# One decoder step on one core: the first projection with features on the partitions and 320 moving tokens, turned back by transposes

## The chip, the cores and the metric

The kernel runs on one core of a Trainium2 chip. The metric is device time in microseconds (us), the median of several executions; lower is better. One more execution was taken with the hardware profiler, and all rows below are from it. The engines are PE (TensorE; its weight loads are listed apart as PEld), DVE (VectorE), ACT (ScalarE), POOL (GpSimd) and SP (SyncE, which here only issues DMAs).

## What is computed

One layer of a hybrid decoder for 256 prompt tokens and 8 x 8 sample tokens, 320 in all. The first step is the normalised input times `w_in`; attention, a recurrent branch, the merge and a gated feed-forward network follow.

```python
p = rms_norm(x, norm_g) @ w_in
p_q, p_cmp, p_sel, p_win, p_gate, p_shift, p_merge = jnp.split(p, _splits(PROJ_SIZES), axis=-1)
q = partial_rope(rms_norm(p_q.reshape(B, T, N_HEADS, HEAD_DIM), q_gain), pos)
kv_cmp = kv_rows(p_cmp, k_gains[0], pos)      # likewise kv_sel, kv_win
gates = jax.nn.sigmoid(p_gate.reshape(B, T, N_HEADS, 3))
```

The change concerns the first 2608 columns of `w_in`: q (1024), the three key/value parts (512 each) and the gates (48). Queries and keys are normalised and rotated per head, along the features of a token, so this kernel wants them with tokens on the partitions.

## The kernel before

The stage is `project_qkv`. The columns are cut into 11 chunks, ten of 256 columns and the last (chunk 10) of 48 (`width`). The contraction of 2048 is cut into 16 slices of 128 (`KD`), four to a group, so chunk c has the groups 4c to 4c+3, 44 in all. A group is 128 x 4 x 256 numbers of `w_in`, 512 KB. It goes through the class `Parts`, which has four slots: SP loads it (`load`, L218), ACT rounds it to `hi` (`round`, L224), DVE makes the remainder `lo` (`cut`, L228), PE multiplies. A product in fp32 quality is three matmuls, hi x hi, and the two mixed ones (`three_passes`, L340). The order of each engine is that of its code; semaphores hold it back: a load waits for the `cut` that freed its slot four groups earlier, a `round` for its load and for the matmuls of the group four earlier (`used`), a `cut` for its `round`, and PE for the `cut` of the group (`split`). In the first chunk DVE also normalises the input, slice by slice, into `nH` and `nL` (L356, L361), and PE waits for those slices.

The tokens are the stationary operand: for each of the three token tiles (128, 128, 64, `TOK`) and each of four slices, three matmuls move 256 weight columns, 36 matmuls to a group. The results lie as token rows in banks 3(c%2) + t. ACT's `take(c)` copies the three of them into `pkv` (L556), or, for chunk 10, puts them through the sigmoid into `gates` (L558), after it has rounded the groups of chunk c+1. For the seven chunks in `NORMED` DVE then does `norm_and_rotate` (L595 to L609), and ACT gives the square root in the middle of it (`root`, L562); DVE does this after its cuts of chunk c+1.

SP loads the groups in order; behind group 12 it issues eight copies from DRAM to DRAM (L524, some 1 MB each, `cache_kv_win` into the output), and after the last load `store_rows` writes the key/value rows out, each part after its chunks are taken and rotated; the last part (win) is ten DMAs (L510, L517). The stage ends with a barrier of all engines: SP comes to it after its stores have landed. The stage behind it (`prompt_setup`) begins with DMAs of SP (L648) and copies of POOL (L711).

The product as the changed kernel makes it stands in the kernel already, as `tile_pair`, for the other projections: weights stationary (128 of their columns), all 320 tokens moving, 24 matmuls to a group of 256 columns. Its results have features on the partitions.

Of the kernel before, what the change touches and what calls it, by code (L numbers as in the profile page):

```python
# [44 lines left out]
P = 128  # L45
# [93 lines left out]
class Steps:  # L139
# [10 lines left out]
    def turn(self):  # L150
        assert self.cursor == len(self.names), self.names[self.cursor:]
        self.cursor = 0
# [93 lines left out]
def _layer(nc, a, o, top):  # L246
# [7 lines left out]
    def sem(name):  # L254
        s = scope[0].enter_context(nc.semaphore(name))
        if scope[0] is early:
            early_sems.append(s)
        return s

    def settled(eng):  # L260

        eng.sem_inc(passed, 1)
# [220 lines left out]
    def project_qkv():  # L483
        v = Carve(work, w.at)
        sqr = v(3, 4, HD)
        ss, rt, rs = v(3, 4), v(3, 4), v(3, 4)
        rope = v(4, 3, 4, 8)
        normed, halved, lowered = sem("n1_normed"), sem("n1_halved"), sem("n1_lowered")
        taken, cleared, low_out = sem("qkv_taken"), sem("qkv_cleared"), sem("qkv_low_out")
        norm_sq, rooted, ready, stored = sem("qkv_sq"), sem("qkv_root"), sem("qkv_ready"), sem("qkv_stored")  # L490
        wv = a["w_in"].rearrange("l (k p) c -> p (l k) c", p=P)
        NCH = 11
        NORMED = (0, 1, 2, 3, 4, 6, 8)

        def width(c):
            return 256 if c < 10 else 48

        with nc.Block() as block:
            @block.sync
            def _(sp):  # L500
                def store_rows(j):

                    name = ("cmp", "sel", "win")[j]
                    sp.wait_ge(ready, 5 + j)
                    sp.wait_ge(taken, 3 * (6 + 2 * j))
                    for t, (t0, n) in enumerate(TOK):
                        src = pkv[0:n, t, ATT + j * KVC:ATT + (j + 1) * KVC]
                        if t < 2:
                            dst = o["kv_%s_prompt" % name][0, 0, t0:t0 + n].rearrange("t c g d -> t (c g d)")
                            sp.dma_start(dst, src).then_inc(stored, 16)  # L510
                        elif name != "win":
                            dst = o["kv_%s_sample" % name].rearrange("l b t c g d -> (l b t) (c g d)")
                            sp.dma_start(dst, src).then_inc(stored, 16)
                        else:
                            for b in range(DB):
                                dst = o["kv_win_sample"][0, b, WIN - TS:WIN].rearrange("t c g d -> t (c g d)")
                                sp.dma_start(dst, src[b * TS:(b + 1) * TS, :]).then_inc(stored, 16)  # L517

                for g in range(4, 4 * NCH):
                    c, n = g // 4, width(g // 4)  # L520
                    parts.load(sp, 0, g, wv[:, g % 4 * 4:g % 4 * 4 + 4, c * 256:c * 256 + n], n)
                    if g == 12:
                        for b in range(DB):
                            sp.dma_start(o["kv_win_sample"][0, b, 0:WIN - TS].rearrange("t c g d -> t (c g d)"),  # L524
                                         a["cache_kv_win"][0, b, TS:WIN].rearrange("t c g d -> t (c g d)")).then_inc(win_stores, 16)
                for j in range(3):
                    store_rows(j)
                sp.wait_ge(stored, 16 * (3 * 2 + 2 + DB))
                sp.wait_ge(win_stores, 16 * DB)

            @block.tensor
            def _(pe):
                parts.start_use(pe)
                for g in range(4 * NCH):
                    c, n = g // 4, width(g // 4)
                    parts.ready(pe, 0, g)
                    if g < 4:
                        pe.wait_ge(lowered, 4 * g + 4)
                    if g % 4 == 0 and c >= 2:

                        pe.wait_ge(taken, 3 * (c - 1))
                    for t, (t0, m) in enumerate(TOK):
                        for kk in range(4):
                            k = g % 4 * 4 + kk
                            last = three_passes(bank[3 * (c % 2) + t][0:m, 0:n], parts.hi[:, g % 4, kk, 0:n], parts.lo[:, g % 4, kk, 0:n],
                                                nH[:, k, t0:t0 + m], nL[:, k, t0:t0 + m], False, k == 0, k == KD - 1)
                    last.then_inc(parts.used, 1)

            @block.scalar
            def _(act):  # L550
                def take(c):
                    parts.done(act, 0, 4 * c + 3)
                    for t, (t0, m) in enumerate(TOK):
                        src = bank[3 * (c % 2) + t][0:m, 0:width(c)]
                        if c < 10:
                            nc.scalar.copy(pkv[0:m, t, c * 256:(c + 1) * 256], src).then_inc(taken, 1)  # L556
                        else:
                            nc.scalar.activation(gates[0:m, t, :], src, ACT.Sigmoid).then_inc(taken, 1)  # L558

                def root(c):  # L560
                    act.wait_ge(norm_sq, NORMED.index(c) + 1)
                    nc.scalar.activation(rt, ss, ACT.Sqrt, bias=const("eps")[:, 0:1], scale=1.0 / HD).then_inc(rooted, 1)  # L562

                norm_high(act, parts, full1, normed, halved)
                act.wait_ge(cleared, 1)
                for c in range(NCH):

                    for g in range(4 * c, 4 * c + 4) if c else ():
                        parts.round(act, 0, g, width(c))
                    if c >= 1:  # L570
                        take(c - 1)
                        if c - 1 in NORMED:
                            root(c - 1)
                take(NCH - 1)

            @block.gpsimd
            def _(pool):

                nc.gpsimd.memset(pkv[64:P, 2, :], 0.0).then_inc(cleared, 1)
                pool.dma_start(x_kept, xT[:, :, :]).then_inc(low_out, 16)  # L580
                pool.wait_ge(lowered, KD)
                pool.dma_start(low_dram, nL[:, :, :]).then_inc(low_out, 16)
                pool.wait_ge(low_out, 32)

            @block.vector
            def _(dve):
                own = Chain(dve, sem("qkv_dve"))
                tt = nc.vector.tensor_tensor
                norm_parts(dve, parts, full1, nL, "norm1_g", rstd1, normed, halved, lowered)

                def norm_and_rotate(c):
                    n = NORMED.index(c)
                    dve.wait_ge(taken, 3 * c + 3)
                    x = pkv[:, :, c * 256:(c + 1) * 256].rearrange("p t (h d) -> p t h d", d=HD)
                    own(tt(sqr, x, x, ALU.mult))  # L595
                    nc.vector.tensor_reduce(ss, sqr, AX.X, ALU.add).then_inc(norm_sq, 1)
                    dve.wait_ge(rooted, n + 1)
                    own(nc.vector.reciprocal(rs, rt))
                    own(tt(x, x, rs.unsqueeze(3).to_broadcast([P, 3, 4, HD]), ALU.mult))
                    gain = gains[:, max(n - 3, 0):max(n - 3, 0) + 1, :].unsqueeze(2).to_broadcast([P, 3, 4, HD])  # L600
                    own(tt(x, x, gain, ALU.mult))
                    cos, sin = (const("rope", 3, 2, 8)[:, :, j:j + 1, :].to_broadcast([P, 3, 4, 8]) for j in range(2))
                    x1, x2 = x[:, :, :, 0:8], x[:, :, :, 8:16]
                    own(tt(rope[:, 0], x1, cos, ALU.mult))
                    own(tt(rope[:, 1], x2, sin, ALU.mult))
                    own(tt(rope[:, 2], x2, cos, ALU.mult))
                    own(tt(rope[:, 3], x1, sin, ALU.mult))
                    own(tt(x1, rope[:, 0], rope[:, 1], ALU.subtract))
                    tt(x2, rope[:, 2], rope[:, 3], ALU.add).then_inc(ready, 1)  # L609
                    dve.wait_ge(ready, n + 1)  # L610

                for c in range(NCH):
                    for g in range(4 * c, 4 * c + 4) if c else ():
                        parts.cut(dve, 0, g, width(c))
                    if c - 1 in NORMED:
                        norm_and_rotate(c - 1)

    project_qkv()
    products.close()
# [2151 lines left out]
```

## Time and profile before

| | us |
|---|---|
| median of 3 executions | 3189.82 |
| lowest, highest | 3187.14, 3193.31 |
| the profiled execution, its time | 3192.92 |
| its span in the trace | 3191.1 |
| first matmul of `project_qkv` | 57.51 |
| last one starts | 262.81 |
| SP's first DMA behind the barrier | 263.78 |

The profiled execution has 1.8 us outside the span and lies 3.1 us above the median. PE is busy for 90% of the span, DVE 45%, ACT 30%, POOL 14%. Busy shares are means over stages of different kinds, so the part below goes through the stage itself: when each engine does what, and what it had waited for. Times in the rows are us from the start of the span; a matmul's own duration is longer than the step from one matmul to the next, since they are pipelined, so steps are read from starts.

### The profile page before, as it was taken

To read this page: it belongs to the slowest core of one execution; us is meant where nothing else is said; L and a number is where in the kernel's file an instruction comes from. 1 tells how busy PE (TensorE), PEld (TensorE's weight loads), DVE (VectorE), ACT (ScalarE), POOL (GpSimd) and SP (SyncE) were. 2 spreads that over 40 slices of the span, in tenths; PEclk is the share of its full clock that TensorE was granted. 3 is DMA by queue.
4 is the path that set the end of the run, shared out by engine and by line. 5 is a ranking of instruction groups with operands and counts; after the bars stand their busy time and mean duration, and the time that the engine had idled before them with its cause. 6 is when DMAs were issued, how large, how long until landed. Compare 5 with 4: busy or idle time off the path is not lost. (4 is left out here: it accounts for less than half of the span.)

```text
span 3191.1 us, 52572 instructions
## 1 busy us (share of the span) xinstructions
PE 2874.9 (90%) x18491; PEld 2449.2 (77%) x18491; DVE 1424.1 (45%) x2693; ACT 959.1 (30%) x1914; POOL 441.6 (14%) x584
## 2 busy tenths in 40 slices
PE   6898878887869969999999979898999989999999
PEld 4896654444449958778777857576999989999999
DVE  4542432423325435555555521005666643566643
ACT  3223322222223333333333311002444333344332
POOL 0000013422400013332332300000000000000000
PEclk9995558888879979999999989998999999999999
DMA  5730016546436512222222254432545444444453
GB/s 171 236 108 10 0 53 192 164 145 183 146 122 180 142 33 64 61 66 63 64 60 64 65 166 148 131 118 79 152 140 155 137 140 151 133 153 146 126 161 111
DMA packets 369287, 378.21 MB, mean 119 GB/s; under 512 B 37114, under 2 KB 329037, under 8 KB 367897
## 3 DMA queue, kind: packets, MB, share of 16 engines
q1 hardware_dynamic: 363444, 359.23, 38.2%
q0 software_dynamic: 1296, 13.11, 1.1%
q10 hardware_dynamic: 4438, 4.40, 0.5%
q8 instruction: 71, 1.16, 0.2%
q14 instruction: 38, 0.31, 0.0%
HBM read 356.99 MB, written 27.94 MB: 121 GB/s over the span
## 5 line engine op out<-in xcount | busy, mean ns | idle before, releaser
L228 DVE TENSOR_TENSOR ffn_lo<-ffn_raw,ffn_hi 128x1024 fp32r<-128x1024 f32 x264 | 319.6, 1223 | 366.1 <-ACT ffn_hi L224 365.8
L340 PE MATMUL banks<-n_hi,ffn_hi 128*128 128x320 f32 x1408 | 437.6, 311 | 15.9 <-DVE ffn_lo L228 15.8
L224 ACT CAST ffn_hi<-ffn_raw 128x1024 fp32r<-128x1024 f32 x264 | 275.6, 1048 | 557.7 <-PE banks L340 525.2
L340 PE MATMUL banks<-n_lo_ffn,ffn_hi 128*128 128x320 f32 x1408 | 436.3, 310 | 0.0
L340 PE MATMUL banks<-n_hi,ffn_lo 128*128 128x320 f32 x1408 | 436.2, 310 | 0.0
L340 PEld LDWEIGHTS banks<-n_hi,ffn_hi 128*128 128x128 f32 x1408 | 265.4, 189 | 17.5 <-issue 17.3
L340 PEld LDWEIGHTS banks<-n_lo_ffn,ffn_hi 128*128 128x128 f32 x1408 | 265.5, 189 | 0.0
L340 PEld LDWEIGHTS banks<-n_hi,ffn_lo 128*128 128x128 f32 x1408 | 265.4, 188 | 0.0
L340 PE MATMUL banks<-g_hi,ffn_hi 128*128 128x320 f32 x704 | 220.0, 313 | 13.5 <-DVE ffn_lo L228 13.5
L2010 POOL TENSOR_TENSOR gate_low<-work,gate_high 128x512 fp32r<-128x512 f32 x128 | 166.8, 1304 | 462.4 <-ACT gate_high L1889 462.4
L340 PE MATMUL banks<-g_lo,ffn_hi 128*128 128x320 f32 x704 | 219.1, 311 | 0.0
L340 PE MATMUL banks<-g_hi,ffn_lo 128*128 128x320 f32 x704 | 219.1, 311 | 0.0
L340 PE MATMUL banks<-n_hi,gate_high 128*128 128x320 f32 x512 | 187.2, 366 | 19.5 <-ACT work L1894 18.7
L340 PE MATMUL banks<-qkv_hi,n_hi 128*128 128x256 f32 (+3 forms) x528 | 151.9, 288 | 18.3 <-DVE qkv_lo L228 18.3
L340 PE MATMUL banks<-n_lo_shift,gate_high 128*128 128x320 f32 x512 | 160.0, 312 | 0.0
L340 PE MATMUL banks<-n_hi,gate_low 128*128 128x320 f32 x512 | 160.0, 312 | 0.0
L2330 PE MATMUL banks<-work,ring_out 128*128 128x320 f32 x512 | 140.3, 438 | 14.0 <-DMA ring_out<-w_out 14.0
L340 PE MATMUL banks<-qkv_lo,n_hi 128*128 128x256 f32 (+3 forms) x528 | 151.6, 287 | 0.0
L340 PE MATMUL banks<-qkv_hi,n_lo_qkv 128*128 128x256 f32 (+3 forms) x528 | 151.4, 287 | 0.0
L340 PEld LDWEIGHTS banks<-g_hi,ffn_hi 128*128 128x128 f32 x704 | 133.7, 190 | 14.0 <-issue 14.0
L2330 PEld LDWEIGHTS banks<-work,ring_out 128*128 128x128 f32 x512 | 98.5, 193 | 55.8 <-issue 16.0
L340 PEld LDWEIGHTS banks<-g_lo,ffn_hi 128*128 128x128 f32 x704 | 133.7, 190 | 0.0
(389 smaller groups left out, 5734.3 us busy)
## 6 DMA issues: line engine op xcount, KB each, us to landing
ffn_raw<-w_up SPq DMA_DIRECT2D x176, 512.0 KB, 3.7
ffn_raw<-w_down SPq DMA_DIRECT2D x88, 512.0 KB, 3.6
ring_attention<-cache_kv_sel SPq DMA_DIRECT2D x128, 256.0 KB, 2.9
work<-w_in SPq DMA_DIRECT2D x128, 256.0 KB, 2.9
work<-cache_kv_cmp SPq DMA_DIRECT2D x96, 256.0 KB, 2.9
shift_raw<-w_in SPq DMA_DIRECT2D x48, 512.0 KB, 3.7
qkv_raw<-w_in SPq DMA_DIRECT2D x40, 512.0 KB, 4.2
ring_out<-w_out SPq DMA_DIRECT2D x16, 1024.0 KB, 5.3
```

The lines of the kernel that those rows point to most:

```text
L224: self.nc.scalar.copy(self.hi[:, j % 4, :, 0:n], self.raw[:, j % 4, :, 0:n]).then_inc(self.rounded, 1)
L228: self.nc.vector.tensor_tensor(self.lo[:, j % 4, :, 0:n], self.raw[:, j % 4, :, 0:n], self.hi[:, j % 4, :, 0:n].bitcast(F32), ALU.subtract ...
L340: ins = nc.tensor.matmul(out, lhs, rhs, start=first and n == 0, stop=last and n == 2)
L2010: nc.gpsimd.tensor_tensor(gate_low[n % 4][:, :, :], gate_raw[n % 4], gate_high[n % 4][:, :, :].bitcast(F32), ALU.subtract).then_inc(gate_c ...
L2330: last = nc.tensor.matmul(bank[g][:, 0:NT], slots[:, c, k, h * P:(h + 1) * P], mT[:, c % 2 * 8 + k, :], start=c % 2 == 0 and k == 0, stop= ...
```

## The change

Chunks 0 to 9 are multiplied with `tile_pair` into banks 0 to 3 (two for each chunk), 24 matmuls of 320 columns to a group. Chunk 10 takes 12 matmuls to a group, 48 weight columns stationary and 320 tokens moving. ACT's new `hold(c)` copies the two feature tiles into `byfeat`; PE's new `turn(c)` transposes them, six transposes to a chunk, into banks 4 to 7; ACT's `take(c)` then makes two copies from there instead of three (128 x 2 x 256 and 64 x 256). PE does `turn(c)` after the matmuls of chunk c+1. ACT and DVE do `take`, `root` and `norm_and_rotate` of a chunk one chunk later than before.

```diff
             def _(pe):
                 parts.start_use(pe)
-                for g in range(4 * NCH):
...
-                    for t, (t0, m) in enumerate(TOK):
-                        for kk in range(4):
-                            k = g % 4 * 4 + kk
-                            last = three_passes(bank[3 * (c % 2) + t][0:m, 0:n], parts.hi[:, g % 4, kk, 0:n], parts.lo[:, g % 4, kk, 0:n],
-                                                nH[:, k, t0:t0 + m], nL[:, k, t0:t0 + m], False, k == 0, k == KD - 1)
-                    last.then_inc(parts.used, 1)
+                def turn(c):
+                    pe.wait_ge(held, c + 1)
+                    if c >= 2:
+                        pe.wait_ge(taken, 2 * (c - 1))
+                    settled(pe)
+                    m = min(P, width(c))
+                    for i in range(2 if c < 10 else 1):
+                        for t, (t0, n) in enumerate(TOK):
+                            out = bank[4 + c % 2][0:n, 256 * t + P * i:256 * t + P * i + m] if t < 2 else bank[6 + c % 2][0:n, P * i:P * i + m]
+                            last = nc.tensor.transpose(out, byfeat[0:m, c % 2 * 2 + i, t0:t0 + n], ident[0:m, 0:m])
+                    last.then_inc(turned, 1)
+
+                for c in range(NCH):
+                    for g in range(4 * c, 4 * c + 4):
+                        if g < 4:
+                            pe.wait_ge(lowered, 4 * g + 4)
+                        if g % 4 == 0 and c >= 2:
+                            pe.wait_ge(held, c - 1)
+                        if c < 10:
+                            tile_pair(pe, parts, 0, g, bank[2 * (c % 2):2 * (c % 2) + 2], nL)
+                        else:
...
+                                last = three_passes(bank[0][0:48, 0:NT], parts.hi[:, g % 4, kk, 0:48], parts.lo[:, g % 4, kk, 0:48],
+                                                    nH[:, k, :], nL[:, k, :], True, k == 0, k == KD - 1)
...
+                    if c:
+                        turn(c - 1)
+                turn(NCH - 1)
             @block.scalar
+                def hold(c):
+                    parts.done(act, 0, 4 * c + 3)
+                    m = min(P, width(c))
+                    for i in range(2 if c < 10 else 1):
+                        last = nc.scalar.copy(byfeat[0:m, c % 2 * 2 + i, :], bank[2 * (c % 2) + i][0:m, 0:NT])
+                    last.then_inc(held, 1)
+
                 def take(c):
-                    parts.done(act, 0, 4 * c + 3)
...
+                    act.wait_ge(turned, c + 1)
...
                     if c >= 1:
-                        take(c - 1)
-                        if c - 1 in NORMED:
-                            root(c - 1)
+                        hold(c - 1)
+                    if c >= 2:
+                        take(c - 2)
+                        if c - 2 in NORMED:
+                            root(c - 2)
+                hold(NCH - 1)
+                take(NCH - 2)
                 take(NCH - 1)
             @block.vector
-                    if c - 1 in NORMED:
-                        norm_and_rotate(c - 1)
+                    if c - 2 in NORMED:
+                        norm_and_rotate(c - 2)
             @block.sync
-                    sp.wait_ge(taken, 3 * (6 + 2 * j))
+                    sp.wait_ge(taken, 2 * (6 + 2 * j))
```

How the rows stand on DVE, at the passage from chunk 0 to chunk 2, before: `L228` is a cut, `L595` and `L596` begin `norm_and_rotate(0)`.

```order
L228 TENSOR_TENSOR qkv_lo<-qkv_raw,qkv_hi 128x1024 [waits parts_rounded] x5
L595 TENSOR_TENSOR work<-work 128x768 [waits qkv_taken]
L596 TENSOR_REDUCE work<-work 128x12 [waits qkv_dve]
L598 RECIPROCAL work<-work 128x12 [waits qkv_root]
L599 TENSOR_TENSOR work<-work 128x3x256 [waits qkv_dve]
```

The same place after:

```order
L228 TENSOR_TENSOR qkv_lo<-qkv_raw,qkv_hi 128x1024 [waits parts_rounded] x9
L628 TENSOR_TENSOR work<-work 128x768 [waits qkv_taken]
L629 TENSOR_REDUCE work<-work 128x12 [waits qkv_dve]
L631 RECIPROCAL work<-work 128x12 [waits qkv_root]
L632 TENSOR_TENSOR work<-work 128x3x256 [waits qkv_dve]
```

The cuts of groups 3 to 7 stood ahead of the first normalisation; now those of groups 3 to 11 do, the cut of group 8 among them.

PE after, at the end of the stage, where the last matmuls of chunk 10 are followed by `turn(9)` and `turn(10)` (L546), and the barrier comes:

```order
L340 MATMUL banks<-n_lo_qkv,qkv_hi 48x320
L340 MATMUL banks<-n_hi,qkv_lo 48x320
L546 MATMUL banks<-cst,work 128x128 [waits qkv_held,qkv_taken]
L546 MATMUL banks<-cst,work 128x128
L546 MATMUL banks<-cst,work 64x128
L546 MATMUL banks<-cst,work 128x128 x2
L546 MATMUL banks<-cst,work 64x128
L546 MATMUL banks<-cst,work 128x48 [waits qkv_held,qkv_taken]
L546 MATMUL banks<-cst,work 128x48
L546 MATMUL banks<-cst,work 64x48
L500 UNCONDITIONAL_BRANCH
```

Before, nothing stood between the last matmul of chunk 10 and the barrier.

ACT after, at the same place: `root(8)`, `hold(10)`, `take(9)` in two copies, then the table of the sigmoid and `take(10)`.

```order
L591 ACTIVATE work<-work,cst 128x12 [waits qkv_sq]
L575 COPY work<-banks 48x320 [waits parts_used]
L583 COPY work<-banks 128x2x256 [waits qkv_turned]
L584 COPY work<-banks 64x256
L586 ACT_TABLE_LOAD
L586 ACTIVATE work<-banks 128x96 [waits qkv_turned]
```

Before, `take(9)` stood right behind the last cast of chunk 10, ahead of the table load, and needed only the matmuls of chunk 9; now it stands behind `hold(10)`, which waits for the last matmul of all.

## Rows read from the trace of the kernel before

**Rows 1.** Windows: length; busy us (instructions) of PE, PEld, DVE, ACT, POOL; granted clock; DMA share, GB/s.

```profile
72.90:115.50 42.60, 42.60 (x361) 42.34 (x360) 21.61 (x31) 9.78 (x16) 0.00 (x0) 1.00 0.88 298
...
124.70:128.00 3.30, 3.29 (x15) 3.29 (x16) 2.64 (x3) 2.19 (x5) 0.00 (x0) 0.50 0.96 280
128.00:240.60 112.60, 112.60 (x961) 112.60 (x959) 57.38 (x82) 31.98 (x50) 0.00 (x0) 1.00 0.41 119
...
244.00:263.00 19.00, 19.00 (x109) 18.97 (x108) 0.00 (x0) 0.00 (x0) 0.00 (x0) 0.50 0.06 14
...
273.90:278.00 4.10, 4.10 (x14) 1.96 (x14) 0.00 (x0) 2.58 (x9) 0.00 (x0) 0.50 0.02 0
635.00:645.00 10.00, 10.00 (x25) 2.44 (x23) 4.51 (x3) 0.00 (x0) 4.48 (x4) 1.00 0.00 0
```

**Rows 2.** Waits from 57.5 to 264: in total, times, longest.

```profile
ACT qkv_hi L224 <- PE banks L340: 73.8, 24, 3.9
ACT qkv_hi L224 <- DMA qkv_raw<-w_in: 32.0, 4, 22.4
```

**Rows 3.** Timeline of ACT: start, duration, then what it had waited for.

```profile
207.91 0.90 ACT L556 COPY work<-banks 128x256 f32<-128x256 f32 x3
211.18 1.05 ACT L224 CAST qkv_hi<-qkv_raw 128x1024 fp32r<-128x1024 f32 x1 [2.38 <-PE banks L340]
215.42 1.05 ACT L224 CAST qkv_hi<-qkv_raw 128x1024 fp32r<-128x1024 f32 x1 [3.18 <-PE banks L340]
...
1054.69 1.05 ACT L224 CAST shift_hi<-shift_raw 128x1024 fp32r<-128x1024 f32 x1 [2.47 <-PE banks L340]
1058.21 1.05 ACT L224 CAST shift_hi<-shift_raw 128x1024 fp32r<-128x1024 f32 x1 [2.47 <-PE banks L340]
```

**Rows 4.** Timeline of PE where transposes stand in a stream of matmuls.

```profile
3072.44 0.31 PE L340 MATMUL banks<-g_hi,ffn_lo 128*128 128x320 f32 x1
3072.59 0.81 PE L2646 MATMUL banks<-cst,oT 128*128 128x128 f32 x6
3073.16 0.39 PE L340 MATMUL banks<-g_hi,ffn_hi 128*128 128x320 f32 x1
3073.39 0.31 PE L340 MATMUL banks<-g_lo,ffn_hi 128*128 128x320 f32 x1
```

**Rows 5.** Timelines of ACT, DVE, SP and PE around the stall.

```profile
87.41 1.99 ACT L224 CAST qkv_hi<-qkv_raw 128x1024 fp32r<-128x1024 f32 x2
...
122.36 1.04 ACT L224 CAST qkv_hi<-qkv_raw 128x1024 fp32r<-128x1024 f32 x1 [22.44 <-DMA qkv_raw<-w_in]
...
71.66 4.63 DVE L228 TENSOR_TENSOR qkv_lo<-qkv_raw,qkv_hi 128x1024 fp32r<-128x1024 f32 x4 [0.46 <-ACT qkv_hi L224]
84.08 1.23 DVE L228 TENSOR_TENSOR qkv_lo<-qkv_raw,qkv_hi 128x1024 fp32r<-128x1024 f32 x1 [7.78 <-ACT qkv_hi L224]
...
91.54 3.50 DVE L228 TENSOR_TENSOR qkv_lo<-qkv_raw,qkv_hi 128x1024 fp32r<-128x1024 f32 x3
...
93.20 5.19 SPq L524 DMA_DIRECT2D out_kv_win_sample<-cache_kv_win  x8
...
124.71 0.58 PE L340 MATMUL banks<-qkv_hi,n_hi 128*128 128x256 f32 x1 [9.18 <-DVE qkv_lo L228]
```

**Rows 6.** Timeline of SP at the end of the stage.

```profile
242.06 0.81 SPq L510 DMA_DIRECT2D out_kv_win_prompt<-work  x2
242.92 3.49 SPq L517 DMA_DIRECT2D out_kv_win_sample<-work  x8
263.78 0.72 SPq L648 DMA_DIRECT2D work<-w_cmp  x1
```

**Rows 7.** Waits of SP from 240 to 264.5, at the same place.

```profile
SPq L498 <- DMA out_kv_win_sample<-work: 1.1, 1, 1.1
```

**Rows 8.** Transposes elsewhere, by line: duration ns min/median/max, first and last start.

```profile
L675 PE MATMUL banks<-cst,work x12: 366/421/477, 273.9 to 277.3; 128*128 128x128 f32 x8, 64*128 64x64 f32 x4
...
L2646 PE MATMUL banks<-cst,oT x48: 270/273/330, 3072.6 to 3183.6; 128*128 128x128 f32 x32, 128*64 128x128 f32 x16
```

More of the change, by code:

```diff
@@ L487, in project_qkv @@
         rope = v(4, 3, 4, 8)
+        byfeat = v(4, NT)
+        held, turned = sem("qkv_held"), sem("qkv_turned")
         normed, halved, lowered = sem("n1_normed"), sem("n1_halved"), sem("n1_lowered")
@@ L533, in _ @@
                 parts.start_use(pe)
-                for g in range(4 * NCH):
[L535 to L541, printed above, removed]
-                    for t, (t0, m) in enumerate(TOK):
-                        for kk in range(4):
-                            k = g % 4 * 4 + kk
-                            last = three_passes(bank[3 * (c % 2) + t][0:m, 0:n], parts.hi[:, g % 4, kk, 0:n], parts.lo[:, g % 4, kk, 0:n],
-                                                nH[:, k, t0:t0 + m], nL[:, k, t0:t0 + m], False, k == 0, k == KD - 1)
-                    last.then_inc(parts.used, 1)
+                def turn(c):
[9 more added lines that the diff above has]
+                    last.then_inc(turned, 1)
@@ new lines, in _ @@
+                for c in range(NCH):
[7 more added lines that the diff above has]
+                        else:
+                            parts.ready(pe, 0, g)
+                            for kk in range(4):
+                                k = g % 4 * 4 + kk
+                                last = three_passes(bank[0][0:48, 0:NT], parts.hi[:, g % 4, kk, 0:48], parts.lo[:, g % 4, kk, 0:48],
+                                                    nH[:, k, :], nL[:, k, :], True, k == 0, k == KD - 1)
+                            last.then_inc(parts.used, 1)
+                    if c:
+                        turn(c - 1)
@@ L549, in _ @@
+                turn(NCH - 1)
             @block.scalar
             def _(act):
-                def take(c):
-                    parts.done(act, 0, 4 * c + 3)
[L553 to L558, printed above, removed]
+                def hold(c):
[4 more added lines that the diff above has]
+                    last.then_inc(held, 1)
@@ new lines, in take @@
+                def take(c):
+                    act.wait_ge(turned, c + 1)
+                    n = width(c)
+                    first = bank[4 + c % 2][:, :].rearrange("p (t f) -> p t f", t=2)[:, :, 0:n]
+                    if c < 10:
+                        nc.scalar.copy(pkv[:, 0:2, c * 256:(c + 1) * 256], first).then_inc(taken, 1)
+                        nc.scalar.copy(pkv[0:NS, 2, c * 256:(c + 1) * 256], bank[6 + c % 2][0:NS, 0:n]).then_inc(taken, 1)
+                    else:
+                        nc.scalar.activation(gates[:, 0:2, :], first, ACT.Sigmoid).then_inc(taken, 1)
+                        nc.scalar.activation(gates[0:NS, 2, :], bank[6 + c % 2][0:NS, 0:n], ACT.Sigmoid).then_inc(taken, 1)
@@ L592, in norm_and_rotate @@
                     n = NORMED.index(c)
-                    dve.wait_ge(taken, 3 * c + 3)
+                    dve.wait_ge(taken, 2 * c + 2)
                     x = pkv[:, :, c * 256:(c + 1) * 256].rearrange("p t (h d) -> p t h d", d=HD)
```

## The prediction

> **What bounds the kernel now.** I read the windows of the stage first, for which engine has no idle time. From 72.9 to 115.5 and again from 128.0 to 240.6 PE is busy all the time at full clock (2.4 GHz), DVE for about half of it, ACT for less than a third [rows 1]. The waits say the same from the other side: ACT waits 73.8 us for PE in 24 places [rows 2]. So in these stretches a step off PE's stream is a step off the time. Two places are different. ACT waits 32.0 us for loads, 22.4 us of it in one place [rows 2]: group 13 of the weights lies behind the eight DRAM copies that SP issues at 93.20, lands at 122.36, and PE idles 9.18 us for it until 124.71 [rows 5]; I call this the stall. And up to 72.9 DVE is the bound: it normalises the input and makes the cut of group 3 at 71.66 + 1.23 = 72.9 [rows 5], so groups 0 to 2 gain nothing by a faster product. From 244 on the clock is at half (1.2 GHz), with 48 columns moving in each matmul [rows 1]. SP's next DMA behind the barrier at 263.78 [rows 6] marks the end of the stage, from where all that follows should run as before, only earlier.
>
> **The steps on PE.** The casts of ACT follow PE's groups: 215.42 - 211.18 = 4.24 us for 36 matmuls of 256 columns, 117.6 ns each [rows 3]. The new form runs in another stage already: 1058.21 - 1054.69 = 3.52 us for 24 matmuls of 320 columns, 146.7 ns each [rows 3]. A group saves 0.71 us, a chunk of four 2.9. The product of columns fell from 9216 to 7680 a group, by 17%, and the time by the same. A `turn` costs six transposes. The same six stand in the last stage in the midst of such matmuls: from the matmul at 3072.44 to the second one behind them at 3073.39 there are 0.95 us, of which two matmul steps are 0.29, so they add 0.66 us [rows 4]. At half clock the transposes of L675 follow one another in about 3.4 us / 11 = 0.31 us [rows 8], which makes 1.9 us for six; that is the upper end, and I take 0.66, since the neighbours are the same matmuls at the same clock. A chunk is then 4 x 3.52 + 0.66 = 14.7 us against 16.9.
>
> The Trainium skill ("TensorE: Matmul & The Clock Gate", Back-to-back issue gap) gives a warm matmul N/2.4 + 2.5 ns: 109 ns for 256 columns and 136 for 320. By it a group would save 0.67 us and not 0.71, one microsecond less over 27 groups; the trace has both steps some 8% longer, and it decides.
>
> **Do ACT and DVE keep up?** ACT's part of a chunk: four casts of 1.05, `hold` of two copies of 320 columns (the old 256-column ones take 0.90 / 3 = 0.30 [rows 3], so about 0.8), `take` of the old 768 columns 0.9, and a wait for the norm's first half, some 2.7: 8.6 us of 14.7. DVE's: four cuts of 1.23, and a normalisation that lies between the cuts at 84.08 and 91.54, so 91.54 - 85.3 = 6.3 us [rows 5]: 11.2 us of 14.7. The tightest place: counted from the last matmul of chunk c-1, ACT casts group 4c+3, holds and takes until 2.9, DVE rotates until 9.2 and cuts group 4c+4 until 10.4; PE wants it at 14.7. So 4 us to spare. `turn(c)` wants a `hold` done 12 us earlier. These copies and waits I cost at nothing; should the cover go, each us over the 4 costs one us on each of seven chunks.
>
> **The stall** is a DMA matter: the copies start when SP has issued load 12, which waits for the cut of group 8. Before, that cut stood behind `norm_and_rotate(0)` and began at 91.54; the issue came right behind, at 92.8, the copies at 93.20 [rows 5]. Now it stands ahead of it. The cut of group 7 ends at 85.3 as before (its load lands late, and PE has work: group 7's turn comes at 72.9 + 4 x 3.52 = 87.0). ACT is through with cast 7 and `hold(0)` at 84.9, so cast 8 can end at 86.0 and cut 8 at 87.2, 5.6 us earlier than before. Its load, though, is only known to have landed by 87.41, when ACT cast it after another wait [rows 5]; that late, the gain would be 3.1. From the issue of the copies to group 13's landing went 29.2 us, and I take that as fixed, but load 11 now flows beside the start of the copies (512 KB at the 298 GB/s of that stretch [rows 1], up to 1.7 us). So between 1.4 and 5.6; I take 5.0, near the upper end: the load of group 8 was free to go right behind the cut of group 4, the second of the four from 71.66 to 76.3 [rows 5], so it had some ten us. The stall then ends at 119.7. PE runs dry at 72.9 + 10 x 3.52 + 2 x 0.66 = 109.4, so it idles 10.3 us: what PE gains ahead of the stall beyond the 5.0 us is lost in it.
>
> **From the stall to the last matmul of chunk 9.** 27 groups, before from 124.71 to 240.6, 115.9 us. The clock is at half for the first 3.3 us [rows 1], which costs 1.65 either way. After: 27 x 3.52 + 1.65 + six turns x 0.66 = 100.6, so 15.3 us less.
>
> **The end.** Before, 240.6 to 263.8 is 23.2 us: 144 short matmuls, most at half clock [rows 1]. After: `turn(8)` 0.66, then 48 matmuls of 320 columns. I price them at 146.7 ns, 7.0 us; at half clock they would take (3.3 us / 15 = 0.22 us for 256 columns [rows 1], so 0.27 for 320) 13.0. Behind them stands a **new tail**. SP's last ten stores need `take(9)`, which now waits for `hold(10)` and `turn(9)`: 0.7 us behind the last matmul plus 0.9 of its own. Then SP issues ten DMAs, 242.06 to 246.41, 4.35 us [rows 6], waits 1.1 for the last to land [rows 7], and the barrier takes 0.3. That is 0.66 + 7.0 + 1.6 + 4.35 + 1.1 + 0.3 = 15.0 us. (`norm_and_rotate(8)` ends about 8.5 us behind the last matmul of chunk 9, ahead of the stores; table load, `turn(10)` and sigmoids, some 4 us, lie beside SP's 5.5.) Gain 8.2. Before, these stores lay under PE's slow matmuls; a version that takes chunk 9 earlier would win some 5 us more.
>
> **Sum:** 5.0 + 15.3 + 8.2 = 28.5 us. From the profiled execution: 3192.9 - 28.5 = 3164.4; the median of the runs lies 3.1 lower, so **3161.3**. The executions of before spread by 3 us to each side.
>
> **Rivals.**
> A, the stall's end does not move: the copies are bound by the DMA from an earlier point than their issue, or load 8 lands late. For it: the DMA share was 0.88 over the whole stretch [rows 1]. Against it: the copies cannot move before they are issued. 5.0 us of the gain go: 3166.3.
> B, chunk 10 runs at half clock, as in the rows of before. For it: only 48 of the array's columns hold weights. Against: from 635 to 645 PE runs a stream at 1.00 whose matmuls (L1024 in the kernel) have 32 stationary columns and 512 moving [rows 1]. Price 6.0: 3167.3.
> C, the slow side: the transposes between the matmuls bring the clock to half, and the chunks behind them run at it. A run of transposes alone does stay there: from 273.9 to 278 PE is busy all the time at 0.50 [rows 1], 421 ns each against 273 for those of L2646 [rows 8]. At half clock a chunk is 96 x 0.27 + 1.9 = 27.8 us, 13.1 more than I forecast; the 28.5 us are gone after 2.2 such chunks of nine. All nine would give 3161 + 118 = 3279. Against it: six transposes amid the matmuls are 0.66 us and the step behind them is back at 0.15 us [rows 4].
> The Trainium skill states the ground for C (the same page, Part 4: PE-mode transpose): transposes do not count as activity for the clock. The row at 273.9 agrees; the trace of the mixed stream does not show a loss.
> D, the later `take` and `root` hold up DVE and so PE: slack 4 us; at 1 us over it, on seven chunks, 3168.
> E, more is gained: load 8 is in time and nothing is added to the copies, or the clock recovers earlier behind the shorter stretch: 3158.
>
> **Numbers.** Forecast 0.70, A 0.10, B 0.07, C 0.04, D 0.04, E 0.05. 0.2% is 6.4 us, about what a measurement of this kernel can tell from no change. All but C, and a stronger D, lie beyond it: faster 0.94, same 0.02, slower 0.04. The range holds the forecast with the runs' own spread, E, and A and B: 3154 to 3171.
>
> **What the trace after would show.** Starts of L224 casts 3.52 us apart within a chunk from 140 on, PE busy throughout at clock 1.00; one `turn` every 14.7 us, its first matmul behind it 0.2 us late; the DRAM copies issued near 87.6 and the stall ending near 120; 48 steps of 147 ns in chunk 10; SP's stores beginning some 1.6 us behind the last matmul, and the barrier at 235.3. I am wrong if casts come 4.2 us apart, if PE waits for a cut at the start of a chunk, if the clock column falls below 1.00 behind a `turn`, or if a later stage gives the time back.

## The result and the profile after

| | before | changed |
|---|---|---|
| median us | 3191.36 (4 runs, 3187.14 to 3193.31) | 3163.66 (4 runs, 3161.01 to 3165.77) |
| ratio | | 0.9911, 95% interval 0.9899 to 0.9924 |
| profiled execution: its time, its span | 3192.92, 3191.1 | 3165.77, 3163.9 |
| stage, from the first matmul of group 3 to SP's first DMA behind the barrier | 72.94 to 263.78: 190.84 | 72.60 to 235.78: 163.18 |

The forecast was 3161.3, the measured time is 2.4 us above it and in the range; the gain is 27.7 us, forecast 28.5. So 0.8 of the 2.4 us are the sum's, and 1.5 come from the kernel before, whose median is 3191.36 with a fourth execution, where the forecast started from 3189.82. The stage has 27.66 us of the gain, so nothing worth naming was given back behind it: the span ran on for 2927.3 us behind the barrier before and 2928.1 after. That stage and median agree so closely is partly chance: in the eleven profiled executions of this document the part behind the barrier, where the kernels do the same, lasted from 2922.7 to 2930.7 us. Differences of a few us between two kernels are therefore read from the stage. I count it from the first matmul of group 3, which waits for DVE in every version, because that matmul comes between 71.80 and 73.36 us in these executions.

One execution of the kernel of e4 below was a slow one, with 4670.72 us, and the row of e4 counts the other three alone (3160.80 to 3163.59).

The windows of the changed kernel, in the columns of [rows 1], show the stretch ahead of the stall, the half clock behind it, the stretch up to chunk 9's end, and chunk 10 with the turns around it:

```profile
72.60:109.40 36.80, 36.76 (x252) 36.48 (x252) 16.21 (x20) 9.97 (x15) 0.00 (x0) 1.00 1.01 345
119.00:124.00 5.00, 4.98 (x19) 4.98 (x20) 4.27 (x4) 2.64 (x6) 0.00 (x0) 0.50 0.93 275
124.00:220.40 96.40, 96.40 (x667) 96.36 (x667) 56.17 (x81) 35.42 (x56) 0.00 (x0) 1.00 0.45 133
220.40:228.20 7.80, 7.80 (x57) 6.55 (x56) 5.43 (x10) 2.04 (x6) 0.00 (x0) 1.00 0.00 1
```

Behind the stall PE is busy without a gap, at 1.00 from 124.3 on, through all the chunks with their turns, and in chunk 10 too, where [rows 1] had 0.50. ACT's casts, which follow PE's groups, stand 3.52 us apart against 4.24 in [rows 3]:

```profile
140.00 1.05 ACT L224 CAST qkv_hi<-qkv_raw 128x1024 fp32r<-128x1024 f32 x1 [2.00 <-PE banks L340]
143.52 1.05 ACT L224 CAST qkv_hi<-qkv_raw 128x1024 fp32r<-128x1024 f32 x1 [2.47 <-PE banks L340]
```

A turn on PE's timeline, `turn(8)` at the passage to chunk 10:

```profile
220.34 0.31 PE L340 MATMUL banks<-n_hi,qkv_lo 128*128 128x320 f32 x1
220.49 0.82 PE L546 MATMUL banks<-cst,work 128*128 128x128 f32 x6
221.06 0.39 PE L340 MATMUL banks<-n_hi,qkv_hi 128*48 128x320 f32 x1
221.29 0.31 PE L340 MATMUL banks<-n_lo_qkv,qkv_hi 128*48 128x320 f32 x1
```

From 220.34 to 221.29 there are 0.95 us, the same as in [rows 4], so a turn adds 0.66 us. Behind it stand the matmuls of chunk 10, 48 stationary columns and 320 moving, in the same steps of 0.147 us.

The stall, to be held against [rows 5]: DVE's cut of group 8, ACT's cast of group 13, SP's copies, PE's first matmul of group 13:

```profile
85.53 1.22 DVE L228 TENSOR_TENSOR qkv_lo<-qkv_raw,qkv_hi 128x1024 fp32r<-128x1024 f32 x1 [1.73 <-ACT qkv_hi L224]
...
116.66 1.04 ACT L224 CAST qkv_hi<-qkv_raw 128x1024 fp32r<-128x1024 f32 x1 [20.45 <-DMA qkv_raw<-w_in]
...
87.19 5.11 SPq L526 DMA_DIRECT2D out_kv_win_sample<-cache_kv_win  x8
...
119.02 0.64 PE L340 MATMUL banks<-n_hi,qkv_hi 128*128 128x320 f32 x1 [9.66 <-DVE qkv_lo L228]
```

The cut of group 8 begins at 85.53, before it was at 91.54 behind the first normalisation; the copies go out at 87.19 instead of 93.20, and ACT casts group 13 29.5 us later, against 29.2. PE idles 9.66 us, against 9.18.

The end of the stage, on ACT and on SP, as [rows 6]:

```profile
228.38 0.42 ACT L575 COPY work<-banks 48x320 f32<-48x320 f32 x1 [3.58 <-PE banks L340]
229.04 0.58 ACT L583 COPY work<-banks 128x512 f32<-128x512 f32 x1 [0.24 <-PE banks L546]
229.52 0.36 ACT L584 COPY work<-banks 64x256 f32<-64x256 f32 x1
229.90 1.28 ACT L586 ACT_TABLE_LOAD   x1
...
229.97 0.81 SPq L512 DMA_DIRECT2D out_kv_win_prompt<-work  x2
230.83 3.35 SPq L519 DMA_DIRECT2D out_kv_win_sample<-work  x8
235.78 1.41 SPq L681 DMA_DIRECT2D work<-w_cmp  x2
```

`hold(10)`, `take(9)`, and then the ten stores; SP has its first DMA of the next stage out 5.8 us behind the beginning of the stores. ACT is through at 231.5, so SP alone holds the barrier.

### The profile page after: what moved, and what is told of

The parts are those of the page before. It is cut to its first block and busy times, and to the rows that moved or that the text cites. A ratio compares the mean times of both kernels' runs of the same rounds, so it can differ in the third digit from the quotient of the medians.

```text
span 3163.9 us, 51569 instructions
## 1 busy us (share of the span) xinstructions
PE 2838.7 (90%) x17978; PEld 2413.4 (76%) x17978; DVE 1432.5 (45%) x2693; ACT 964.9 (30%) x1924; POOL 442.1 (14%) x584
## 5 line engine op out<-in xcount | busy, mean ns | idle before, releaser
L228 DVE TENSOR_TENSOR ffn_lo<-ffn_raw,ffn_hi 128x1024 fp32r<-128x1024 f32 x264 | 319.5, 1223 | 365.7 <-ACT ffn_hi L224 365.5
L340 PEld LDWEIGHTS banks<-g_hi,ffn_lo 128*128 128x128 f32 x704 | 133.6, 190 | 0.0
L2572 POOL COPY ffn_work<-ffn_work 128x2 f32<-128x2 f32 x88 | 23.1, 262 | 781.0 <-ACT ffn_work L2543 543.2
L340 PE MATMUL banks<-n_hi,shift_hi 128*128 128x320 f32 x400 | 124.9, 312 | 7.4 <-DVE shift_lo L228 7.4
```

Of the source, the lines that this page charges most:

```text
L228: self.nc.vector.tensor_tensor(self.lo[:, j % 4, :, 0:n], self.raw[:, j % 4, :, 0:n], self.hi[:, j % 4, :, 0:n].bitcast(F32), ALU.subtract ...
L340: ins = nc.tensor.matmul(out, lhs, rhs, start=first and n == 0, stop=last and n == 2)
L2572: nc.gpsimd.tensor_copy(dst[:, 0:2], ub[:, u, T:T + 2])
```

## The experiments

Each was compared with the kernel before on the same chip, whose median was 3191.58 beside e1 to e4, 3193.07 beside e5 to e8 and 3192.23 beside e9; so the ratios compare better than the medians. The stage lengths are from the profile of each:

| kernel | median us | ratio to before (95%) | stage us |
|---|---|---|---|
| before | | | 190.84 |
| changed | 3163.66 | 0.9911 (0.9899 to 0.9924) | 163.18 |
| e1 norm later, old product | 3184.93 | 0.9979 (0.9969 to 0.9989) | 185.50 |
| e2 turns four times | 3177.54 | 0.9955 (0.9938 to 0.9971) | 179.00 |
| e3 chunk 10 as before | 3179.16 | 0.9965 (0.9953 to 0.9978) | 177.59 |
| e4 turn(9) early | 3161.55 | 0.9905 (0.9886 to 0.9925) | 161.38 |
| e5 before, copies spread | 3182.06 | 0.996 (0.9946 to 0.9974) | 178.23 |
| e6 changed, copies spread | 3152.72 | 0.9869 (0.9852 to 0.9885) | 151.17 |
| e7 e6 with turns in the next chunk | 3150.8 | 0.9863 (0.9846 to 0.9879) | 151.64 |
| e8 turns in the next chunk, copies together | 3164.89 | 0.9913 (0.9897 to 0.993) | 168.21 |
| e9 e6 with the last two chunks early | 3147.55 | 0.9858 (0.9842 to 0.9874) | 148.51 |

### e1: only the later normalisation

```diff
                         take(c - 1)
-                        if c - 1 in NORMED:
-                            root(c - 1)
+                    if c >= 2 and c - 2 in NORMED:
+                        root(c - 2)
...
-                    if c - 1 in NORMED:
-                        norm_and_rotate(c - 1)
+                    if c - 2 in NORMED:
+                        norm_and_rotate(c - 2)
```

> The kernel before, with only one thing of the change: root and norm_and_rotate of a chunk come one chunk later (take stays). Theory: the stall ends when the DRAM copies have flowed, 29 us behind their issue, and the issue hangs on the cut of group 8, which now stands ahead of the first normalisation. So copies near 87.2 to 87.6 instead of 93.2, PE's stall ends near 119 instead of 124.7 and is about 3.5 us long instead of 9.2, stage end 258 instead of 263.8, time 5 to 6 us less, all without tile_pair. Rival A (the landing of group 13 is bound by traffic that was there before the copies were issued): copies issued earlier, stall end still near 124, time unchanged.

Measured: 5.3 us off the stage. DVE's timeline has the cuts of groups 7, 8 and 9 with nothing between them, SP's and PE's follow:

```profile
83.30 1.23 DVE L228 TENSOR_TENSOR qkv_lo<-qkv_raw,qkv_hi 128x1024 fp32r<-128x1024 f32 x1 [7.78 <-ACT qkv_hi L224]
85.05 2.50 DVE L228 TENSOR_TENSOR qkv_lo<-qkv_raw,qkv_hi 128x1024 fp32r<-128x1024 f32 x2 [0.52 <-ACT qkv_hi L224]
...
86.71 5.09 SPq L524 DMA_DIRECT2D out_kv_win_sample<-cache_kv_win  x8
...
118.69 0.58 PE L340 MATMUL banks<-qkv_hi,n_hi 128*128 128x256 f32 x1 [3.92 <-DVE qkv_lo L228]
```

The stall ends at 118.69 with the old, slower product just as with the new one, 6.0 us earlier than before, and is 3.9 us long. So the end of the stall is set by the issue of the copies, and the 5 us of the changed kernel there come from DVE's order, not from PE. Rival A has fallen.

### e2: every transpose four times

```diff
-                    for i in range(2 if c < 10 else 1):
+                    for i in [*range(2 if c < 10 else 1)] * 4:
```

> The changed kernel with every transpose of turn made four times into the same place, 24 to a turn. Theory (six transposes amid the matmuls cost 0.66 us and nothing else): 2.0 us more for each turn; turns 0 and 1 vanish in the stall, turns 2 to 8 and 9 stand on the path, so 8 x 2.0 = 16 us more than the changed kernel, clock 1.00 throughout the chunks. Rival C (transposes pull the clock down): with 2.6 us of transposes in each chunk the clock column falls below 1.00 behind the turns, a chunk takes well over 16.7 us, and the time rises by 40 us or more.

Measured: 15.8 us more on the stage, 13.9 on the median. The windows from 128 on, and one turn:

```profile
128.00:236.00 108.00, 108.00 (x781) 107.92 (x780) 53.51 (x75) 35.38 (x56) 0.00 (x0) 1.00 0.39 114
...
166.21 0.31 PE L340 MATMUL banks<-n_hi,qkv_lo 128*128 128x320 f32 x1
166.36 2.79 PE L546 MATMUL banks<-cst,work 128*128 128x128 f32 x24
168.90 0.39 PE L340 MATMUL banks<-n_hi,qkv_hi 128*128 128x320 f32 x1
169.13 0.30 PE L340 MATMUL banks<-n_lo_qkv,qkv_hi 128*128 128x320 f32 x1
```

24 transposes add 2.92 - 0.29 = 2.63 us, 18 more than six add 1.97, 0.11 us each. The clock stays at 1.00 behind 2.5 us of nothing but transposes, in every chunk from 128 on. Rival C is out, and with a margin: turns of four times the size don't bring it about.

### e3: chunk 10 in the old form

```diff
-                            for kk in range(4):
-                                k = g % 4 * 4 + kk
-                                last = three_passes(bank[0][0:48, 0:NT], ... nH[:, k, :], nL[:, k, :], True, ...)
+                            for t, (t0, m) in enumerate(TOK):
+                                if g == 40 and t == 2:
+                                    pe.wait_ge(held, 10)
+                                for kk in range(4):
+                                    k = g % 4 * 4 + kk
+                                    last = three_passes(bank[t][0:m, 0:48], ... nH[:, k, t0:t0 + m], ... False, ...)
...
-                turn(NCH - 1)
...
-                hold(NCH - 1)
                 take(NCH - 2)
-                take(NCH - 1)
+                parts.done(act, 0, 4 * NCH - 1)
+                for t, (t0, m) in enumerate(TOK):
+                    nc.scalar.activation(gates[0:m, t, :], bank[t][0:m, 0:48], ACT.Sigmoid).then_inc(taken, 1)
```

> The changed kernel with chunk 10 multiplied as before (tokens stationary, 48 columns moving, 36 matmuls to a group, no turn(10)), turn(9) and take(9) still behind it. Theory: chunk 10 takes 22 us, most at half clock, instead of 7.1, while SP's stores still wait for take(9) behind it: 14 to 15 us more than the changed kernel, stage end near 250.5. Rival: the end of the stage is set by SP's stores and not by PE's last chunk: less than 5 us more.

Measured: 14.4 us more on the stage, 15.5 on the median. Chunk 10's clock, in the columns of [rows 1], and the stores:

```profile
219.00:224.00 5.00, 5.00 (x51) 4.99 (x50) 2.27 (x3) 1.79 (x6) 0.00 (x0) 1.00 0.02 5
224.00:242.00 18.00, 18.00 (x112) 17.96 (x112) 3.69 (x9) 0.25 (x1) 0.00 (x0) 0.55 0.00 1
...
244.02 0.81 SPq L512 DMA_DIRECT2D out_kv_win_prompt<-work  x2
```

So the new form of the last chunk is worth 14.4 us by itself. The end of the changed kernel is 7.9 us shorter than before, so the other 6.5 went to `turn(8)` and to the tail.

### e4: the last take earlier

```diff
+                            if g == 40:
+                                turn(9)
-                    if c:
+                    if c and c < 10:
                         turn(c - 1)
...
-                hold(NCH - 1)
                 take(NCH - 2)
+                hold(NCH - 1)
                 take(NCH - 1)
```

> The changed kernel with turn(9) behind the first group of chunk 10 and take(9) ahead of hold(10). The prediction says that a version that takes chunk 9 earlier would win some 5 us. Against that stands norm_and_rotate(8), whose last instruction in the trace of the changed kernel is about 1 us ahead of the stores, and on which they wait too. Theory 1 (take(9) alone holds the stores): stage end 5 us earlier, near 231. Theory 2 (the norm of chunk 8 is late next): stores begin near 229 instead of 230, stage end 1 us earlier.

Measured: 1.8 us off the stage of the changed kernel, and no difference in the median that could be told. Only 1.0 of the 1.8 us is the tail's: from the last matmul of chunk 9 to the next stage it is 14.3 us instead of 15.3. Of the rest 0.4 lie ahead of the stall's end, and half a us is a shorter stretch at half clock behind it (4.3 us instead of 5.3). The last instruction of `norm_and_rotate(8)` and the first store:

```profile
227.02 0.26 DVE L644 TENSOR_TENSOR work<-work 128x96 f32<-128x96 f32 x1
...
227.31 0.81 SPq L512 DMA_DIRECT2D out_kv_win_prompt<-work  x2
```

`take(9)` was done at 224.0. The stores now wait for the normalisation of chunk 8, theory 2. The 5 us that the prediction names for such a version were wrong: it took one wait away and did not ask what is late next. Its own figures had the answer, with that normalisation ending 8.5 us behind the last matmul of chunk 9 and the stores beginning 0.66 + 7.0 + 1.6 = 9.3 us behind it, 0.8 us apart.

### e5 and e6: the copies spread over the loads

```diff
-                    if g == 12:
-                        for b in range(DB):
+                    if g >= 12 and g % 4 == 0:
+                        for b in (g // 4 - 3,):
```

> The kernel before, with the eight DRAM copies issued one behind each of the groups 12, 16, ..., 40 instead of all behind group 12. Theory (the stall is those copies ahead of group 13's load, and nothing else): no stall (9.2 us) and no half clock behind it (1.65 us), so stage end near 253 instead of 263.8, some 11 us less. Rival: the traffic is the same and only moves, so PE waits 1 to 2 us behind each copy, together about as long: less than 3 us gained.

> The changed kernel with the same spread copies. Theory: no stall (9.7 us) and no half clock (2.5 us), stage end near 223.6 instead of 235.8. Against the kernel before with spread copies that is 29.3 us: 37 groups x 0.71 + last chunk 8.2 - turns 5.9, where the stall no longer levels anything. Rival: with groups of 3.52 us the copies and loads (1 MB and 4 x 0.5 MB in 14.7 us) no longer fit beside PE, and waits for loads of several us remain: stage end above 228.

Measured: 12.6 us off the stage of the kernel before (251.20 at its end), 12.0 off the changed one (224.06). The only load that ACT waited for for long in e6 is that of group 7, which is there in all versions:

```profile
ACT qkv_hi L224 <- DMA qkv_raw<-w_in: 9.6, 4, 7.5
```

Against [rows 2], 22 us of waiting for loads are gone, and PE never runs dry from 72.9 to the end of chunk 10. The two kernels with spread copies are 27.1 us apart, against 27.7 of the two without. The 29.3 of the expectation was added up wrongly, its terms make 26.3 + 8.2 - 5.9 = 28.6. The 1.5 that are missing to that lie in chunk 10 of the old form, which was faster in e5: 21.2 us from ACT's cast at 229.97 to SP's first DMA behind the barrier at 251.20, where the kernel before took 23.0. In e5 the clock fell to 0.50 only 5.4 us behind the first matmul of 48 columns, and in the kernel before 3.5 us behind it. That is also why e5 gained 12.6 us and not the 11 expected.

### e7 and e8: all turns inside the next chunk

```diff
                     for g in range(4 * c, 4 * c + 4):
+                        if c and g == 4 * c + 1:
+                            turn(c - 1)
...
-                    if c:
-                        turn(c - 1)
...
                         hold(c - 1)
-                    if c >= 2:
-                        take(c - 2)
-                        if c - 2 in NORMED:
-                            root(c - 2)
+                        take(c - 1)
+                        if c - 1 in NORMED:
+                            root(c - 1)
                 hold(NCH - 1)
-                take(NCH - 2)
                 take(NCH - 1)
...
-                    if c - 2 in NORMED:
-                        norm_and_rotate(c - 2)
+                    if c - 1 in NORMED:
+                        norm_and_rotate(c - 1)
```

This is all of e8; e7 has the spread copies of e6 as well.

> The changed kernel with spread copies, and turn(c) behind the first group of chunk c+1, so that take, root and norm_and_rotate come one chunk earlier again, as in the kernel before. Theory: the norm of chunk 8 is done in chunk 9, take(9) early in chunk 10, the stores run under chunk 10's matmuls, and the stage ends with turn(10), a table load and the sigmoids some 2 us behind the last matmul: stage end near 219 (4.5 us earlier than with spread copies alone). DVE and ACT have 2 us to spare in each chunk instead of 4. Rival: that slack is not there, PE waits for the first cut of each normalised chunk, and the gain is lost: stage end 224 or later.

> The same order of turn, take and norm, but with all copies behind group 12. It undoes the later norm inside the changed kernel. Theory: the cut of group 8 again stands behind norm_and_rotate(0), copies issued near 92 and stall end near 124 (5 us later than in the changed kernel), and the tail gives back 5: stage end 235 to 236, time equal to the changed kernel within 1 us. Rival (the stall's end hangs on PE's speed, not on the order of DVE): stall end near 119, stage end near 231.

Measured: e7 has the stage of e6 within 0.5 us, where 4.5 us less were expected, and the stage of e8 is 5.0 us longer than that of the changed kernel, where the same was expected. The medians don't show these 5.0 us: e8 has the ratio 0.9913 and the changed kernel 0.9911, and in the profiled executions the part behind the barrier was 5.4 us shorter in e8 (2922.7 against 2928.1), for which no run gives a cause. Both theories missed the same wait. PE's first turn in e7, and its third in e8:

```profile
83.83 0.85 PE L546 MATMUL banks<-cst,work 128*128 128x128 f32 x6 [3.45 <-ACT work L575]
...
127.63 1.51 PE L546 MATMUL banks<-cst,work 128*128 128x128 f32 x6 [13.74 <-ACT work L575]
```

`turn(c)` in the next chunk waits for `hold(c)`, which stands on ACT behind the casts of that chunk; where a load is late, the cast waits for it, the hold behind it, and PE behind the hold, with matmuls ready that it could do. In e7 that is 3.45 us and a clock that falls behind it (0.62 in the window from 86 to 89, 1.00 in e6), in e8 the stall lasts until 127.63 although the copies went out at 93.24, as before. Counted from group 3, the stall of e8 ends 9.1 us later than that of the changed kernel instead of 5. The rest of the theory came: from the last matmul of chunk 9 to the next stage it is 10.2 us in both, 5.1 and 5.4 less than in the changed kernel and in e6. The end of e7, 224.74, is the one that its rival names, but not by the rival's wait: behind 73.1 PE never waits for a cut. That DVE's order decides when the copies go out is seen once more (93.24 against 87.19). The later turn of the change has a use that its code does not show: it keeps PE clear of ACT's waits for loads.

### e9: only the last two chunks early

```diff
+                        if g in (38, 42):
+                            turn(8 if g == 38 else 9)
...
-                    if c:
+                    if c and c < 9:
                         turn(c - 1)
...
-                    if c >= 2:
-                        take(c - 2)
-                        if c - 2 in NORMED:
-                            root(c - 2)
+                    for b in ((c - 2,) if c < 9 else (7, 8) if c == 9 else (9,)):
+                        if b >= 0:
+                            take(b)
+                            if b in NORMED:
+                                root(b)
                 hold(NCH - 1)
-                take(NCH - 2)
                 take(NCH - 1)
...
-                    if c - 2 in NORMED:
+                    if c < 9 and c - 2 in NORMED:
                         norm_and_rotate(c - 2)
+                    if c == 9:
+                        norm_and_rotate(8)
```

> The changed kernel with spread copies, where only the last two chunks are taken earlier: turn(8) inside chunk 9 and turn(9) inside chunk 10, each behind two groups, with take(8), root(8) and norm_and_rotate(8) in chunk 9 and take(9) in chunk 10. All chunks ahead keep the later turn, so that no matmul waits for a hold that stands behind a cast whose load is late, as it did at turn(0) in the version with all turns early. Theory: stores begin some 5 us behind the last matmul of chunk 9 instead of 9.5, stage end near 220 instead of 224.1, set by SP's stores and by the sigmoids within 1 us of one another; time 4 us below the version with spread copies alone, 3149. Rival: a turn inside a chunk makes PE wait for its hold as before, stage end 223 or later.

Measured: 2.7 us off e6's stage, and with 3147.55 the lowest median of all, 45 us and 1.4% below the kernel before; the intervals of e6, e7 and e9 overlap, so that e9 is the fastest is shown by the stage and not by the medians. PE has one wait between 71.80 and chunk 10's end, 0.71 us at the first matmul of chunk 10, whose cut stands behind `norm_and_rotate(8)` on DVE. The gain is 1.3 us smaller than expected: besides that wait, the end of the stage still hangs on SP, whose stores go out at 214.26, 0.1 us behind `take(9)`, which waits for the turn behind the second group. The stage ended at 220.31, 1.4 us behind the last sigmoid.

```profile
208.94 0.32 PE L340 MATMUL banks<-n_hi,qkv_hi 128*48 128x320 f32 x1 [0.71 <-DVE qkv_lo L228]
...
213.80 0.36 ACT L586 COPY work<-banks 64x256 f32<-64x256 f32 x1
...
214.26 0.81 SPq L512 DMA_DIRECT2D out_kv_win_prompt<-work  x2
...
218.71 0.19 ACT L589 ACTIVATE work<-banks 64x48 f32<-64x48 f32 x1
...
220.31 1.41 SPq L685 DMA_DIRECT2D work<-w_cmp  x2
```

## Why the prediction was right

The sum had three terms, all of them in the stage, counted here from the first matmul of group 3. The last term begins behind the last matmul of chunk 9, at 240.56 before and, with `turn(8)`, at 220.49 after:

| term | forecast | measured |
|---|---|---|
| up to the end of the stall | 5.0 | 51.77 - 46.42 = 5.35 |
| stall to the end of chunk 9 | 15.3 | 115.85 - 101.47 = 14.4 |
| chunk 10 and the tail | 8.2 | 23.22 - 15.29 = 7.9 |
| sum | 28.5 | 27.7 |

**The steps on PE** were right to the hundredth: 3.52 us a group, 0.66 a turn, both taken from rows of other stages where the same instructions stood in the same company [rows 3, 4]. e2 shows that the turn is on the path and costs what it lasts. The first matmul behind a turn is followed by the next after 0.23 us, 0.08 more than a step, and not 0.2 us late as the prediction has it.

**The stall.** That the place where it ends is decided by DVE's order, and not by how fast PE is, was the step most open to doubt, and e1 shows it alone. The 5.0 us were a choice within bounds of 1.4 and 5.6, and part of the good fit is luck. The prediction kept the cut of group 7 where it was, until 85.3, but that load came 1.5 us earlier (cast at 81.49, before at 83.00). Load 8 was late by a little (cast at 84.44, after 1.25 us of waiting). So the copies went out 6.0 us earlier, 5.7 counted from group 3, and group 13 was cast 29.5 us behind them instead of 29.2.

**From the stall to chunk 9** the gain was 0.9 us smaller. The half clock behind the stall lasted from 119.02 to 124.3 and not 3.3 us as in [rows 1]; 5.3 - 3.3 = 2.0 us more at half speed cost 1.0. In e1 it lasted until 123.7, 5.0 us. The step that was mis-sized is the one that took the length of this stretch over from one execution.

**The end** was right in its parts: chunk 10 at full clock, 7.1 us, then `take(9)` 1.7 us behind the last matmul's end, SP's 4.2 us of issues and some 1.6 until the next stage. e3 shows the two sides of it, 14.4 gained by the form and 6.5 lost to `turn(8)` and the tail. Rival B did not come.

**Rival C** did not come, and e2 tested it at four times the size. **Rival D** did not come in the changed kernel: apart from the stall, every chunk up to the end shows PE without a wait. The argument against it was incomplete, though. It reckoned the slack from durations alone and left ACT's waits for loads out; e7 and e8, with the turn one chunk closer, fell into just that. **The remark on 5 us** for an earlier `take(9)` was wrong: e4 gained 1.0 in the tail.

## What to carry to other kernels

Where the tokens can move and the weights stand still, a product in 320-column steps saves what the columns save (17% here), and turning its result back with six transposes a chunk takes back 0.66 us of the 2.9 us a chunk, as long as they stand among matmuls at full clock. Before a faster engine is credited with time, look for what a stall's end hangs on: here it hung on when the eight DRAM copies were issued, and that on the order of another engine. And put the step that hands back a result where its producer does not stand behind a load: one chunk later cost nothing in the middle of the stage and kept PE clear of a wait of 3.45 us ahead of the stall and of an idle time of 13.7 us instead of 9.7 in it, while the last chunks want it as early as they can get it.

## What the runs showed of the hardware

With 48 columns moving and 128 (or 64) standing, PE was busy throughout and its granted clock was at 0.50 for most of chunk 10 (e3 as in [rows 1]); it fell 3.5, 5.1 and 5.4 us behind the first such matmul, in the kernel before, e3 and e5. With 48 standing and 320 moving it stayed at 1.00 (window 220.40 to 228.20), for the 7.1 us that this chunk lasts; a longer stretch of that form was not run. It stayed there too behind 24 transposes in a row among matmuls (e2), while a stretch of transposes and short work from 273.9 to 278 in the kernel before ran at 0.50 [rows 1], where the clock had been since 244.0. The Trainium skill ("TensorE: Matmul & The Clock Gate", Part 4: PE-mode transpose) says that transposes do not count as a busy PE in the way that matmuls do; e2 neither contradicts that nor shows it, since 14 us of matmuls stood between its turns.

The half clock behind the stall lasted 3.3 us in the kernel before, 5.3 in the changed one, 5.0 in e1, 6.1 in e2, 4.4 in e3, 4.3 in e4 and 6.0 in e8. It does not follow the length of the stall: PE had idled 9.2 us in the first, 5.5 in e2 and 13.7 in e8. What sets it stays open.

With the eight DRAM copies of 1 MB together, group 13 behind them was cast 29.2 us after their first issue in the kernel before, 29.5 in the changed one and 29.0 to 29.6 in e1 to e4 and e8, whatever PE and DVE did meanwhile.
